# A paged decode attention stage rewritten as one stream of 153 turns

## The reference

```python
def diff_attend(q, q_pos, k, v, k_pos, lam):
    s = jnp.einsum('bqhcd,bkhcd->bhcqk', q, k).astype(jnp.float32) * (QK_HEAD ** -0.5)
    mask = k_pos[None, :] <= q_pos[:, None]
    s = jnp.where(mask, s, -jnp.inf)
    p = jax.nn.softmax(s, axis=-1)
    a = p[:, :, 0] - lam * p[:, :, 1]
    return jnp.einsum('bhqk,bkhd->bqhd', a, v.astype(jnp.float32))
...
k_past = cache_k[l, page_table].reshape(bs, past, N_HEADS, 2, QK_HEAD)
v_past = cache_v[l, page_table].reshape(bs, past, N_HEADS, V_HEAD)
```

## Time and profile before

| | us |
|---|---|
| median of 3 runs (2254.36 to 2262.54) | 2258.97 |
| the profiled execution | 2256.54 |
| its span | 2254.7 |
| stages 1 and 2 (adaLN, input projection) | 0 to about 422 |
| stage 3 (attention), from the first gather | 430.5 to 1222 |
| stages 4 and 5 | 1222 to 2254.7 |

### The profile page before, as it was taken

One profiled execution on the slowest core, in us unless ns is written; L12 is line 12 of the kernel. 1 busy time (PEld: TensorE's weight loads), 2 busy tenths in 40 slices (PEclk: granted clock), 3 DMA queues, 4 the chain that ended last, 5 costly groups with the idle time before them and its releaser, 6 DMA issues.

```text
span 2254.7 us, 40461 instructions
## 1 busy us (share of the span) xinstructions
PE 1795.3 (80%) x17492; PEld 1469.9 (65%) x17492; DVE 1056.0 (47%) x1532; ACT 488.1 (22%) x831; POOL 319.0 (14%) x287
## 2 busy tenths in 40 slices
PE   5799999566665766666665994999999999799991
PEld 2277899545554554555454893777777777799991
DVE  2324121476776775767662557112111111465567
ACT  0211111012212122121221104111112110344441
POOL 0000000123232422324322005200000000000003
PEclk8899999677987988879885996999999999899996
DMA  9701123577988989879877310121121121621112
GB/s 310 279 24 51 38 82 123 193 253 300 409 335 322 414 334 414 329 324 414 346 324 299 113 43 13 57 72 59 56 93 56 59 72 37 226 84 40 47 36 96
DMA packets 133284, 404.41 MB, mean 179 GB/s; under 512 B 12153, under 2 KB 76665, under 8 KB 100338
## 3 DMA queue, kind: packets, MB, share of 16 engines
q0 software_dynamic: 37392, 270.55, 29.7%
q1 hardware_dynamic: 87426, 127.52, 16.7%
q10 hardware_dynamic: 8320, 4.19, 0.7%
HBM read 377.79 MB, written 24.51 MB: 178 GB/s over the span
## 4 chain that ended last, share of the span: by engine, by line
PE 63%; DVE 18%; DMA 12%; issue 5%; ACT 1%; DVEq 0%; POOL 0%; SPq 0%; ACTq 0%
PE psum L746 27%; PE psum L995 11%; PE psum L754 10%; DMA k_ring<-cache_k,page_idx 7%; DVE k_turned L1433 6%; DMA ada_w<-w_ada 3%; PE psum L845 2%; PE psum L855 2%; DVE p_t L427 2%; PE psum L729 2%; PE psum L825 1%; DVE x_lo L1278 1%; DMA v_ring<-cache_v,page_idx 1%; PE psum L874 1%; DVE soft L1384 1%
## 5 line engine op out<-in xcount | busy, mean ns | idle before, releaser
L1433 DVE STREAM_TRANSPOSE k_turned<-k_ring 128x2048 f32<-128x2048 f32 x128 | 295.5, 2308 | 7.2 <-DMA k_ring<-cache_k,page_idx 6.9
L746 PE MATMUL psum<-x_hi,w_hi 128*128 128x512 f32 x896 | 281.3, 395 | 0.0
L746 PE MATMUL psum<-x_lo,w_hi 128*128 128x512 f32 x896 | 277.2, 391 | 0.0
L845 PE MATMUL psum<-k_turned,q_blocks 128*32 128x128 f32 x4096 | 157.6, 301 | 150.0 <-DVE k_turned L1433 149.8
L746 PE MATMUL psum<-x_hi,w_lo 128*128 128x512 f32 x896 | 275.9, 389 | 0.0
L1297 DVE TENSOR_TENSOR w_lo<-w_raw,w_hi 128x2048 fp32r<-128x2048 f32 x37 | 86.9, 2350 | 361.9 <-ACT w_hi L1053 352.6
L845 PEld LDWEIGHTS psum<-k_turned,q_blocks 128*32 128x32 f32 x4096 | 117.4, 119 | 205.4 <-issue 153.8
L995 PE MATMUL psum<-d_hi,h_hi 128*128 128x256 f32 x704 | 203.1, 288 | 12.0 <-DVE d_lo L1647 10.7
L995 PE MATMUL psum<-d_lo,h_hi 128*128 128x256 f32 x704 | 200.3, 285 | 0.0
L995 PE MATMUL psum<-d_hi,h_lo 128*128 128x256 f32 x704 | 200.2, 284 | 0.0
L746 PEld LDWEIGHTS psum<-x_hi,w_hi 128*128 128x128 f32 x896 | 165.6, 188 | 44.8 <-issue 5.3
(11 more groups left out here) (228 smaller groups left out, 2503.9 us busy)
## 6 DMA issues: line engine op xcount, KB each, us to landing
ada_w<-w_ada SPq DMA_DIRECT2D x12, 2048.0 KB, 9.0
w_raw<-w_in SPq DMA_DIRECT2D x12, 1024.0 KB, 5.3
w_raw<-w_gate SPq DMA_DIRECT2D x11, 1024.0 KB, 5.4
w_raw<-w_up SPq DMA_DIRECT2D x11, 1024.0 KB, 6.2
h_store<-h_out SPq DMA_DIRECT2D x11, 1024.0 KB, 7.8
h_all<-h_store SPq DMA_DIRECT2D x11, 1024.0 KB, 8.2
d_raw<-w_down SPq DMA_DIRECT2D x44, 256.0 KB, 3.1
x_rows<-x_prompt SPq DMA_DIRECT2D x2, 2048.0 KB, 17.9
```

Source lines behind the costliest of these rows:

```text
L746: last = mm(psum[:, 2 * ft + c, 0:CH], w[:, s, k, ft * P:(ft + 1) * P], x[:, k, c * CH:(c + 1) * CH], start=k == 0 and j == 0, stop=k == K ...
L845: last = mm(psum[QUAD * h:QUAD * (h + 1), g % 2, 0:GP * QUAD], q_blocks[:, h, d, :], k_turned[:, g % 2, :, h * HD + d * QUAD:h * HD + (d + ...
L1433: v.transpose(k_turned[:, g % 2].rearrange("p j n -> p (j n)"), k_ring[:, g].rearrange("p j n -> p (j n)")).then_inc(k_free, 1)
```

## The change

Stage 3 becomes one list of 153 numbered turns (`SLOTS`) for each engine, all straight code. In turn n come the key group n (of 128), the value group n - 23 (`LAG` = 23), one small piece of the softmax of the sequence whose keys ended last, and one quarter of a prompt tile (turns 6 to 141: per head 2 turns for its start and 32 for its tiles). DVE turns key group n + 1 in turn n, one ahead, and in place: `k_turned` as a buffer is gone, and the ring's slot is free only when PE has scored it. The score rows and the query blocks are doubled, `regroup` works on a quarter at a time (32 copies of 32 x 128 a sequence instead of 8 of 32 x 512 on DVE, the same on ACT), the accumulator and scratch banks move, the tile order becomes 0, 7, 1, 6, 2, 5, 3, 4, and the rows of heads 1 to 3 are fetched from SP instead of ACT. A few semaphores are merged.

```diff
-    GP, RING = 4, 4
-    REVS = z.PAGES // (GP * RING)
+    GP, RK, RV = 4, 4, 4
+    STEP = z.PAGES // GP
+    REVS = STEP // 4
+    NK = z.B * STEP
+    LAG = STEP + 7
+    SLOTS = NK + LAG + 2
+    HEAD0, HEAD_SLOTS = 6, 2 + 4 * z.NT
...
-        TILES = ([i for i in range(NT) if i % 4 in (0, 3)], [i for i in range(NT) if i % 4 in (1, 2)])
+        TILES = [i for pair in zip(range(NT // 2), range(NT - 1, NT // 2 - 1, -1)) for i in pair]
...
-        def regroup(copy, j):
+        def regroup(copy, j, r):
+            got = psum[QUAD * j:QUAD * (j + 1), TURNED, :].rearrange("p (g h a q) -> p g h a q", h=H, a=4, q=8)
             to = p_t[:].rearrange("p (g j) (h q) -> p g j h q", j=4, q=8)
             for a in range(4):
-                last = copy(to[QUAD * a:QUAD * (a + 1), :, j], got[:, :, :, a, :])
+                last = copy(to[QUAD * a:QUAD * (a + 1), 4 * r:4 * (r + 1), j], got[:, :, :, a, :])
...
+            for n in range(NK + LAG):
+                if n < NK:
+                    if n >= RK:
+                        pool.wait_ge(scored, n - RK + 1)
+                    gather(k_pages, k_ring[:, n % RK], k_in[n % RK], n)
+                if n >= LAG:
+                    m = n - LAG
+                    if m >= RV:
+                        pool.wait_ge(v_used, m - RV + 1)
+                    gather(v_pages, v_ring[:, m % RV], v_in[m % RV], m)
...
+            for h in range(1, H):
+                sp.wait_ge(rows_turned, h)
+                fetch_head(sp, h)
             stage_end(sp, 3)
...
+            def key_group(n):
+                pe.wait_ge(k_turned, n + 1)
+                if n >= 2:
+                    pe.wait_ge(s_taken, n - 1)
...
+            def value_group(m):
+                e, g = m // STEP, m % STEP
+                if g == 0:
+                    pe.wait_ge(folded, e + 1)
+                    pe.wait_ge(o_scaled_ready, e)
...
+                if g % 4 == 0:
+                    pe.wait_ge(p_by_act, REVS * e + g // 4 + 1)
+                    pe.wait_ge(p_by_dve, REVS * e + g // 4 + 1)
...
+            def slot(n):
+                b, s = n // STEP, n % STEP
+                if n < NK:
+                    if s == 0:
+                        new_keys(b)
+                    key_group(n)
+                if LAG <= n < NK + LAG:
+                    value_group(n - LAG)
+                if 1 <= b <= B:
+                    if s == 1:
+                        turn_max(b - 1)
+                    elif s == 2:
+                        max_to_rows(b - 1)
+                    elif 4 <= s < 4 + REVS:
+                        turn_p(b - 1, s - 4)
+                    if s == 5:
+                        fold_sums(b - 1)
+                if s == 8 and b >= 2:
+                    by_query(b - 2)
+            for n in range(SLOTS):
+                h, u, q = dense_at(n)
...
+                elif q == 0:
+                    if u % NT:
+                        weigh_rows(u - 1)
+                    scores(u, 0)
+                elif q == 1:
+                    scores(u, 1)
+                elif q == 3:
+                    turn_rows(u)
...
+                slot(n)
...
+            def slot(n):
+                b, s = n // STEP, n % STEP
+                if n + 1 < NK:
+                    turn_keys(n + 1)
+                if s == 0 and 1 <= b <= B:
+                    maximum(b - 1)
+                if s == 0 and b < B:
+                    new_scores(b)
+                if b < B:
+                    if s in (4, 8, 12):
+                        turn_maxima(b, s // 4 - 1)
+                    elif s == 10 and b + 1 < B:
+                        queries(b + 1)
+                if 1 <= b <= B:
+                    if s == 1:
+                        spread_max(b - 1)
+                    elif s == 2:
+                        negative_max(b - 1)
+                    elif 4 <= s < 4 + REVS:
+                        keep_p(b - 1, s - 4)
+                    if s == 5:
+                        keep_sums(b - 1)
+                if s == 6:
+                    if b >= 2:
+                        scale_output(b - 2)
+                    if 1 <= b <= B:
+                        keep_scale(b - 1)
```

More of the change, by code:

```diff
@@ L443, in load_pages, with gather @@
         def load_pages(pool):
[L446 to L458, removed]
+            def gather(rows, to, landed, n):
+                pool.indirect_dma_start(to.rearrange("p s d -> p (s d)"), None, rows,
+                                        bass.IndirectOffsetOnAxis(page_idx[:, n:n + 1], 0)).then_inc(landed, 16)
+            for n in range(NK + LAG):
[8 more added lines that the diff above has]
+                    gather(v_pages, v_ring[:, m % RV], v_in[m % RV], m)
         def fetch_head(eng, h):
@@ L883, in by_query @@
[L883 to L890, removed]
-                    turn_head_queries(h)
[L892 to L904, removed]
-                        key_group(b, r, g)
-                        if not first:
-                            value_group(b - 1, r, g, (r, g) == (REVS - 1, RING - 1))
-                    weigh_rows(h, n, i)
-                if not first:
-                    by_query(b - 1)
@@ L912, in _ @@
-            step(0, 0, 0, first=True)
-            with pe.Fori(0, H - 1) as i:
-                step(2 * i + 1, i, 1)
-                step(2 * i + 2, i + 1, 0)
-            step(B - 1, H - 1, 1)
-            softmax(B - 1)
-            for r in range(REVS):
-                for g in range(RING):
-                    value_group(B - 1, r, g, (r, g) == (REVS - 1, RING - 1))
-            by_query(B - 1)
+                        last = mm(psum[QUAD * h:QUAD * (h + 1), ACC, 0:P], p_t[:, g * GP + j, :],
+                                  v_ring[:, m % RV, j, h * HD:(h + 1) * HD], start=False, stop=g == STEP - 1 and j == GP - 1)
@@ new lines, in value_group, with turn_max, max_to_rows @@
+                last.then_inc(v_used, 1)
+            def turn_max(e):
+                pe.wait_ge(max_ready, e + 1)
+                pe.wait_ge(new_added, min(e + 2, B))
+                if e == B - 1:
+                    pe.wait_ge(o_t_kept, e - 1)
+                turn(psum[0:1, MISC, 256:256 + P], dec[:, 0:1], ident).then_inc(max_turned, 1)
+            def max_to_rows(e):
+                pe.wait_ge(max_spread, e + 1)
+                mm(psum[:, MISC, 384:385], max_row[0:1, 1, :], ident[0:1, 0:1], start=True, stop=True).then_inc(max_back, 1)
@@ L1116, in step @@
-            def step(b, h, half, first=False):
-                if not first:
-                    softmax(b - 1)
-                for r in range(REVS):
-                    n, i = b * REVS + r, TILES[half][r]
-                    for g in range(RING):
-                        if g == 3:
-                            keep_turned(n, i)
-                        take_scores(b, r, g)
-                        if g < 2:
-                            exps(n, i, g)
-                if not first:
-                    keep_output(b - 1)
@@ L1130, in _, with keep_p @@
-            step(0, 0, 0, first=True)
-            with act.Fori(0, H - 1) as i:
-                act.wait_ge(rows_turned, i + 1)
-                fetch_head(act, i + 1)
-                step(2 * i + 1, i, 1)
-                step(2 * i + 2, i + 1, 0)
-            step(B - 1, H - 1, 1)
-            softmax(B - 1)
-            keep_output(B - 1)
+            def keep_p(e, r):
+                act.wait_ge(p_turned, REVS * e + r + 1)
+                if e:
+                    act.wait_ge(v_used, STEP * (e - 1) + 4 * (r + 1))
+                for j in range(2):
+                    last = regroup(copy, j, r)
+                last.then_inc(p_by_act, 1)
@@ L1139, in _ @@
+            for n in range(SLOTS):
+                h, u, q = dense_at(n)
+                if q == 3:
+                    keep_turned(u)
+                slot(n)
+                if u is not None and q == 0:
+                    exps(u, 0)
+                elif u is not None and q == 1:
+                    exps(u, 1)
             stage_end(act, 3)
@@ L1467, in step @@
-            def step(b, h, half, first=False):
-                if first:
-                    head_start(h)
-                else:
-                    softmax(b - 1, h if half == 0 else None)
-                queries(b)
-                for r in range(REVS):
-                    n, i = b * REVS + r, TILES[half][r]
-                    for g in range(RING):
-                        turn_keys(b, r, g)
-                        if g == 1 and r:
-                            link(turn_maxima(b, r - 1))
-                        if g < 2:
-                            maxima(n, i, g)
-                        elif g == 2:
-                            combine(n, i)
-                        else:
-                            take_rows(h, n, i)
-                if not first:
-                    scale_output(b - 1)
@@ new lines, in _ @@
+            queries(0)
+            turn_keys(0)
+            for n in range(SLOTS):
```

(18 more changed lines are left out.)

347 lines of the change are left out of this document (192 added, 155 removed).

## The result

The changed kernel takes 2280.9 us (median of 4 runs, 2279.5 to 2287.6) against 2256.7 of the kernel before: a ratio of 1.0113, 95% interval 1.0078 to 1.0149. It is slower by 1.1%. Forecast were 2187 us, with bounds of 2156 and 2232, and 92% for faster.

What follows compares the result with a forecast made beforehand. Bound: transfers and engines taking turns, 73.6 + 22.4 us a step. Turn 23 at 534, 546 us to turn 128, then 45, 22.5 and 2.5 end stage 3 at 1150, not 1222: 72 less, median 2187 us, range 2156 to 2232.

Steps and rivals of the forecast that it cites:

- the third limit of the middle: Turns 23 to 127: way through the tile, DVE to ACT to PE and back, 75 to 78 us per 16 turns.
- the middle: Stage 3, turns 23 to 127, key and value streams together: 5.2 us a turn, 546 us; bounds 5.03 and 5.55.
- The second rival: Chain sets the pace, softmax pieces find no DVE waits: 5.4 to 5.5 us a turn, about 2215 us; chance 0.24.
- The price of the copies: DVE's regrouping in quarters: 6.8 us a sequence, between 5.5 and 8.8, where it now costs 5.5.
- Turns 0 to 22: Stage 3 before the first values: turn 0 at about 439.5, early gathers landing in 5.5 to 6.4 us, turn 23 at 534.
- The ring: Four key slots, each held about 6.8 us instead of some 3; 12 of 20.1 us remain for issue and landing.
- The third rival: Ring of keys too short, decisive from a landing of 15.5 us; at 6.5 us a turn 2324 us; chance 0.05.
- Take-away of the wait in `take_rows`: Prompt tiles: key group turned one turn ahead cuts DVE's wait from 3.6 to about 2 us a tile.
- Straight code, fetching heads from SP, turning in place: Stage 3: no charge for fetching code, head-row fetches free on SP, turning in place 2.31 us as now.
- The alternating order: Tile order in stage 3: makes tile pairs equally long, bounding lateness to one wide tile, about 4 us.
- The rivals' test: Profile signs that the forecast is wrong; for the second rival, middle DMA share 0.9 with DVE above 85% busy.
- the first rival: All hidden behind the transfers: middle 530 us, tail 60, stage 3 ends at 1127, 2164 us; chance 0.18.

Runs made afterwards that it cites:

- the reordered kernel: The changed kernel with the softmax pieces of a turn moved behind the prompt tile's piece on DVE and ACT, no work added or removed: 2195.1 us, ratio 0.9742.
- experiment 7: The reordered kernel with the tiles in the order of the kernel before (0, 3, 4, 7, 1, 2, 5, 6): 2199.2 us, two runs.
- experiment 3: The changed kernel without the prompt's tiles, the decode stream alone, the prompt's attention output a constant: 2158.1 us, one run.

## Why the prediction was wrong, point by point

**The step that failed** is the third limit of the middle, the chain: "the softmax pieces (...) fall half into turns where DVE would have waited, so some 8 remain: 75 to 78, 4.8 us a turn". It priced the pieces as work to be laid into DVE's idle time. The copies are not free to be laid anywhere: each quarter carries a wait for PE's last instructions of the same turn, and behind it on DVE and ACT is queued what PE's next turn begins with. So PE's turn, the copies, the maxima or the combination and the exponentials come one after another in turns 4 to 7 of each sequence, and in a smaller measure in turns 0 to 2, with the maximum and the five exponentials. Sixteen turns took 94.4 us where the step had 75 to 78, and the middle 5.79 us a turn, not 5.2. With the pieces moved back they took 84.3. In the changed kernel turns 23 to 127 are 62 us over the forecast. The same shows in turns 20 to 22, where the first softmax falls (turn 23 is late by 20 us, of which the reordered kernel keeps 10), and behind turn 127 (20 us, of which it keeps 2; most of what it wins there it wins before turn 136). With the pieces moved back and nothing else, the total comes near that of the prediction: 2195 against 2187. That is partly luck, since that kernel starts value groups 10 us late and its copies cost more than I gave them. The second rival had the right place, "between the turning and `maxima`", and the wrong price: it took the work, 13 us a sequence, and no wait, 87 us a sequence and not 94, hence 2215.

**The price of the copies** was too low as well, outside its bounds. After, DVE's group, beside the earlier trace rows:

```profile
L441 DVE COPY p_t<-psum 32x128 f32<-32x128 f32 x256 | 74.5, 291 | 78.5 <-PE psum L920 75.2
```

291 ns each, above the 274 of the copy of 128 partitions that I took as the upper end, and eight take 2.42 us, so they do not overlap at their ends: 9.7 us a sequence where I had 6.8 and at most 8.8. The rows of before had shown no overlap either: eight copies at 0.691 us took 5.62.

**Turns 0 to 22**: turn 0 was forecast at 439.5, with the first group turned. DVE's first turning came at 440.6, after 5.13 us of waiting for the first gather, and PE took key group 0 at 443.0. The 5.5 to 6.4 us that I gave the landing did not hold for the first gather: it was issued at 430.3, 10.3 us before that turning. The reordered kernel is 10 us late at turn 23: 3 of them come from before the stage (its first gather is issued at 433.3), 3.5 from this start, and the other 3.4 are the pace, 97.9 us from key group 0 to the first value product where I had 94.5.

**The ring**: right, but for a small price. 9 us for the late release by itself, and 415 GB/s with it in the stream without tiles. The third rival (landing of 15.5 us or more) did not come; landings in the changed kernel had a median of 10.2 us from 560 to 1180.

**Take-away of the wait in `take_rows`**: forecast from 3.6 to about 2 us a tile; 58.3 us in 32 tiles, 1.8. Right, but PE's wait before `scores` grew from 12.5 to 115.6 us in the same kernel; what the shorter wait is worth by itself was not tested.

**Straight code, fetching heads from SP, turning in place**: nothing against them in the trace; the turning takes 2.30 us as before. The alternating order, on which I leaned for the slack, made no difference (experiment 7).

**The rivals' test** held by half: "a DMA share of 0.9 in the middle" was named as the sign of the chain, and it is 0.92. The other half, DVE above 85% busy, did not come: it is 73%, which is what tells waits from work.

**Small slips**, none of which moves the forecast: the stage's end of the first rival adds up to 1124 (534 + 530 + 60) and not 1127, the low bound to 2159 and not 2156, and step 7 was called saturated, at a share of 0.84 and 335 GB/s.

## What to carry to other kernels

When serial phases are cut up and laid into the turns of a pipeline, cost each piece by what it waits for and by what is queued behind it, not by its length alone: a piece that waits for the end of another engine's turn belongs behind whatever that engine's next turn starts with. Where no engine is busy all the time and no queue of transfers is full, suspect a loop of waits, and look for the instruction whose releaser comes last in the other engine's list. The new order adds no instruction and was worth 86 us here, more than three times the 24 that the whole change had lost.

## What the runs showed of the hardware

Small copies out of PSUM (the memory that PE writes) are dear: 32 x 128 floats take 291 ns on DVE and 254 on ACT against 691 and 574 for 32 x 512, so four quarters cost 1.7 to 1.8 times the whole. A copy of 32 partitions (0.291 us) was not shorter than one of 128 partitions by the same 128 columns (0.271 to 0.274). The gathers held 415 GB/s for 440 us with DVE, ACT and PE at work beside them (experiment 3, one run).
